# Gated linear attention: a head's states, outputs and their norms one level later among the next head's levels

## The reference

```
b      = cumsum(log_a)                                  # inside a chunk
scores = sum_d q[i,d] k[j,d] exp(b[i,d] - b[j,d]), j<=i
o      = scores @ v + (q * exp(b)) @ h                  # h: state at the chunk's start
h_new  = exp(b_last) * h + (k * exp(b_last - b))^T @ v
o      = rms_norm(o) * silu(g)
```

## Time and profile before

| | |
|---|---|
| median of 3 runs | 2581.73 us (2581.23 to 2584.96) |
| profiled execution | 2579.5 us |
| its span | 2577.7 us |
| PE busy | 2478.8 us (96%) |
| DVE busy | 1064.5 us (41%) |
| ACT busy | 520.0 us (20%) |
| POOL busy | 906.9 us (35%) |
| mean granted clock of TensorE | 0.983 |
| passes of head 1, 2 and 3 | 420.3 to 529.0 us of the span |

### The profile page before, as it was taken

How to read it: one execution, slowest core, us unless ns; L and a number is a source line. 1 busy time by engine, 2 the same in 40 slices (tenths; PEclk the granted TensorE clock), 3 DMA queues, 4 the chain that set the end, 5 groups by cost and what they waited for, 6 DMA issues and landing times.

```text
span 2577.7 us, 40356 instructions
## 1 busy us (share of the span) xinstructions
PE 2478.8 (96%) x16293; PEld 2378.6 (92%) x16293; DVE 1064.5 (41%) x1653; ACT 520.0 (20%) x1118; POOL 906.9 (35%) x449
## 2 busy tenths in 40 slices
PE   7899997889999999999999999999999999999998
PEld 6799987779999999999999888678899999999998
DVE  5322226854633333333335554615533333333333
ACT  5322125441200000000002543123200000000000
POOL 4232333523443343343344421300434334334332
PEclk9999998989999999999999999999999999999999
DMA  6111131231111111111111401410111111111112
GB/s 211 44 33 42 50 123 40 76 139 34 58 42 49 49 41 49 49 41 49 49 42 40 167 31 55 140 67 9 50 50 41 49 49 41 49 49 42 47 42 73
DMA packets 41138, 154.53 MB, mean 60 GB/s; under 512 B 4800, under 2 KB 11584, under 8 KB 38864
## 3 DMA queue, kind: packets, MB, share of 16 engines
q1 hardware_dynamic: 33456, 116.49, 13.9%
q10 hardware_dynamic: 7584, 36.63, 3.7%
HBM read 134.77 MB, written 18.33 MB: 59 GB/s over the span
## 4 chain that ended last, share of the span: by engine, by line
PE 89%; DVE 7%; ACT 2%; issue 2%; DMA 0%; POOL 0%; DVEq 0%; ACTq 0%; SPq 0%; POOLq 0%
PE bank L661 26%; PE bank L663 25%; PE bank L662 25%; PE bank L859 2%; DVE x_lo L1853 1%; PE bank L1285 1%; PE bank L687 1%; PE bank L1258 1%; DVE xt L1843 1%; PE bank L1146 1%; PE bank L1255 1%; PE bank L727 1%; PE bank L747 1%; PE bank L1280 1%; PE bank L735 1%
## 5 line engine op out<-in xcount | busy, mean ns | idle before, releaser
L661 PE MATMUL bank<-x_hi,w_hi 128*128 128x344 f32 (+1 forms) x3272 | 1061.6, 324 | 13.5 <-DVE x_lo L1877 5.4
L662 PE MATMUL bank<-x_lo,w_hi 128*128 128x344 f32 (+1 forms) x3272 | 1046.6, 320 | 0.0
L663 PE MATMUL bank<-x_hi,w_lo 128*128 128x344 f32 (+1 forms) x3272 | 1046.6, 320 | 0.0
L542 POOL TENSOR_TENSOR w_hi<-w_raw,zero 128x1024 fp32r<-128x1024 f32 x176 | 339.7, 1930 | 1455.4 <-PE bank L663 1412.1
L661 PEld LDWEIGHTS bank<-x_hi,w_hi 128*128 128x128 f32 x3272 | 618.9, 189 | 26.3 <-issue 22.8
L662 PEld LDWEIGHTS bank<-x_lo,w_hi 128*128 128x128 f32 x3272 | 618.5, 189 | 2.3 <-issue 0.5
L663 PEld LDWEIGHTS bank<-x_hi,w_lo 128*128 128x128 f32 x3272 | 618.6, 189 | 0.0
L544 POOL TENSOR_TENSOR w_lo<-w_raw,w_hi 128x1024 fp32r<-128x1024 f32 x176 | 433.2, 2462 | 13.8
L2192 DVE TENSOR_TENSOR hid<-sil,bank 128x344 f32<-128x344 f32 x132 | 67.5, 512 | 775.5 <-PE bank L663 740.5
L661 PE MATMUL bank<-hid_hi,w_hi 128*128 128x344 f32 x1056 | 339.6, 322 | 1.2 <-issue 1.2
L663 PE MATMUL bank<-hid_hi,w_lo 128*128 128x344 f32 x1056 | 337.6, 320 | 0.0
(11 more groups left out here) (308 smaller groups left out, 1794.9 us busy)
## 6 DMA issues: line engine op xcount, KB each, us to landing
w_raw<-in_w SPq DMA_DIRECT2D x187, 512.0 KB, 3.4
h<-in_x SPq DMA_DIRECT2D x3, 1376.0 KB, 8.5
h_spill<-h ACTq DMA_DIRECT2D x1, 4128.0 KB, 11.5
h<-h_spill ACTq DMA_DIRECT2D x1, 4128.0 KB, 13.6
out_y<-h ACTq DMA_DIRECT2D x3, 1376.0 KB, 5.6
g_spill<-ring ACTq DMA_DIRECT2D x6, 516.0 KB, 2.6
h<-in_x ACTq DMA_DIRECT2D x1, 3096.0 KB, 10.3
st_ring<-in_state SPq DMA_DIRECT2D x4, 768.0 KB, 5.1
```

Source lines behind the costliest of these rows:

```text
L542: nc.gpsimd.tensor_tensor(w_hi[:, s], w_raw[:, s], zero[:].broadcast_to([P, 1024]), ALU.add).then_inc(s_whi, 1)
L661: pe.matmul(out, wh, xh, start=(i == 0), stop=False)
L662: pe.matmul(out, wh, xl, start=False, stop=False)
L663: mm = pe.matmul(out, wl, xh, start=False, stop=(i == n - 1))
```

## The change

In the three hand-written queues the two halves of `outs` and `outs_normed` go from levels 2 and 3 to levels 3 and 4, and those of `states` from levels 1 and 2 to levels 2 and 3. `outs_turned` and `outs_gated` stay.

```diff
@@ PE's queue
-                        if l in (2, 3):
-                            outs(hh - 1, l - 2)
+                        if l in (3, 4):
+                            outs(hh - 1, l - 3)
                         if l in (5, 6):
                             outs_turned(hh - 1, l - 5)
@@ ACT's queue
-                if l in (2, 3) and hh >= 1:
-                    outs_normed(hh - 1, l - 2)
+                if l in (3, 4) and hh >= 1:
+                    outs_normed(hh - 1, l - 3)
@@ DVE's queue
-                    if l in (1, 2) and hh >= 1:
-                        states(hh - 1, l - 1)
+                    if l in (2, 3) and hh >= 1:
+                        states(hh - 1, l - 2)
```

## The result

The changed kernel takes 2584.59 us (median of 20 runs, 2582.08 to 2588.55), the kernel before, run beside it, 2581.02 (20 runs, 2578.03 to 2584.96). The ratio over the runs is 1.0016 with a 95% interval of 1.0009 to 1.0022 (the medians alone give 1.0014): 3.6 us slower, less than the 0.2% that count as a difference here, but not nothing. The forecast was 2584.2 us and 0.81 for "within 0.2%".

A forecast was written before the change was run, and what follows sets the result against it. TensorE is 96% busy, but in the three changed passes a ring of waits between PE, ACT and DVE bounds; +0.8 us at full clock plus 1.65 for one clock drop gives +2.45 on 2581.73: 2584.2 us, range 2579.6 to 2587.3.

The forecast's parts named there:

- The ring: Heads 1 to 3: ACT waits for PE's outputs (20.2 us), DVE for ACT's decays (10.4), PE for DVE's kept scores.
- Head 1: First pass: level 7 comes 2.1 us earlier, less 0.4 for POOL, leaving 1.7 us where head 2 begins.
- Head 2: Second pass: level 2 still waits for decays behind the sample's norm; lead grows to 2.6 us, adding 0.9.
- Head 3: Third pass: level 7 goes from 524.39 to 525.2, as DVE meets POOL's two splits at level 4.
- the lock: Head 3, level 4: DVE's products and POOL's weight splits exclude each other, a price of 3.3 us, bounds 0 and 3.3.
- the laying-out: The new order timed instruction by instruction through heads 1 to 3; level 4's pair in head 3 takes 4.6 us.
- The clock: PE's idle in front of level 3 or 4 lets TensorE drop to 1.2 GHz: 1.65 us taken, bounds 0 and 5.0.
- The likeliest case: DVE and POOL exclude each other in head 3 and one clock drop shows: 2584.2 us, chance 0.32.
- the second case: DVE and POOL exclude each other in head 3 and two clock drops show: 2585.8 us, chance 0.2.
- The price of 1.65: One clock drop: a level with its outputs takes 5.8 us at 1.2 GHz, 4.2 at 2.4, costing 1.65.
- The three heads together: Sign of being right: heads 1 to 3 take 110 to 112 us, not 108.7.
- What stands behind the passes: Stretches outside 420 to 529 us keep their lengths and only shift; a difference there would show the prediction wrong.

The follow-up runs named there:

- e4: Changed kernel with ACT's norms back in the slots of levels 2 and 3, states and outputs still one level later: 2595.38 us, ratio 1.0058.
- e6: Kernel before with only ACT's norms moved, to the slots of levels 3 and 4: 2578.53 us, ratio 0.9990.
- e9: Changed kernel with the sample's norm on ACT behind level 2's decays in heads 2 and 3: 2580.52 us, ratio 1.0003.
- e11: Kernel before with norms one level later, POOL's split late and the sample's norm behind level 2's decays: 2577.07 us, ratio 0.9988.
- e2: Changed kernel with seven of level 2's products made twice on PE in heads 1 to 3: 2582.76 us, ratio 1.0006.
- e3: Changed kernel with seven level 2 products repeated in heads 1 to 3 and POOL's split behind DVE's last product: 2580.51 us, ratio 1.0001.
- e1: Changed kernel with POOL's split of the weight tile held until DVE has made its last product: 2582.79 us, ratio 1.0010.
- e12: Kernel before run again unchanged, for a second profile: 2580.66 us, ratio 0.9999.
- e8: Kernel before with ACT's norms one level later and POOL's split behind DVE's last product: 2576.79 us, ratio 0.9984.
- e10: Changed kernel with the sample's norm behind level 2's decays in heads 2 and 3, and POOL's split behind DVE's last product: 2579.09 us, ratio 0.9998.
- e7: Kernel before with POOL's split behind DVE's last product: 2580.01 us, ratio 0.9998.

## Why the prediction was right

*The ring.* Right, and e4 and e6 show it: in their old slots behind the later outputs the norms cost 10.8 us, and moved alone they gain 2.2 us in each of heads 1 and 2 and 0.3 in head 3. One mark was wrong: I wrote that ACT's wait ahead of L1537 would shrink. It grew to 26.2 us, because the outputs come later too. What matters is what stands behind it in ACT's queue. DVE's wait for L1564 in front of level 5 went in heads 1 and 2, as written, but came back in front of level 6.

*Head 1.* Forecast 1.7 us of lead at full clock, 0.05 with a fall; measured 0.0 (37.98 against 38.01), with the fall. Level 3 was to start at 433.95 and did at 433.71. The 0.4 us taken off for POOL between level 7 and head 2 came out as 0.5 (451.10 to 458.20, and 451.75 to 458.32 before).

*Head 2.* Forecast 0.9 us of gain at full clock, a loss of 0.75 with a fall; measured a loss of 1.0. That the states had been nearly free in the shade of the sample's norm is shown by e9 and e11 together: with the states behind level 2, taking that norm out of the way gains 3.5 us in this head; with the states ahead of level 2 it gains nothing.

*Head 3.* Forecast 3.4 us of loss with the lock at 3.3; measured 3.1 (31.89 against 28.75), and the pair took 4.4 us where the laying-out said 4.6. The lock alone adds 2.7 us from level 3 to level 7 (18.0 in e2, 15.3 in e3), where the laying-out has 2.95 (525.2 less 522.25). But it isn't 2.7 on top of the fall: taking it away gives back only 1.2 (e1), since the fallen clock stands beneath it. One row was misread: L2008's 2.25 us in the earlier trace rows end at 516.18, half a us behind w_lo (515.64), and not just as it was through. The laying-out of level 4 has that half us all the same.

*The clock.* The likeliest case had one visible fall; the profile has two, in heads 1 and 2, and a third beneath the lock. That is the second case, +4.1 us, and level 7 of head 3 is 4.1 us later. The median of 20 runs, +3.6, lies between the two. That the forecast is within 0.4 us of the measured 2584.59 is part luck: the difference was forecast as 2.45 and came out as 3.6, and the 2581.73 it was added to, a median of 3 runs, lies 0.7 above that of 20. The price of 1.65 is right: 1.66 and 1.61 in e2. The number of falls was the uncertain term, and by this profile 0.32 against 0.2 was weighted the wrong way round: I counted the row of 2.10 us without a fall as much as the two with one.

*The three heads together* were to take 110 to 112 us; they take 112.8.

*What stands behind the passes.* I wrote that the other stretches keep their lengths, and that a difference outside 420 to 529 would speak against me. In the two profiles 2.1 of the 6.1 us lie behind level 7 of head 3. I have no account of them from the prediction. The kernel before differs from itself by 1.6 us in such a stretch (e12), so they may be the run's and not the edit's.

*Open.* The leads at level 7 of head 3 are larger than those of the medians: 4.8 us and 1.5 in e6, 6.35 and 3.2 in e8, 4.3 and 0.5 in e10. The stretch between the two products named at e12 runs the same instructions in all kernels and took from 1063.4 us (e6, e12) to 1069.1 (e10), 1066.9 in the changed kernel. Of e10's 4.1 us over the first profile of before, PE's idle time is 1.2; the rest goes with a lower clock, as over these 50 us of the window attention (first before, then e10):

```profile
1650.20:1700.20 50.00, 47.90 (x485) 35.50 (x483) 13.96 (x25) 12.69 (x27) 0.00 (x0) 0.97 0.38 149
```
```profile
1645.00:1695.00 50.00, 47.90 (x453) 35.06 (x450) 14.02 (x25) 11.60 (x25) 0.00 (x0) 0.86 0.37 147
```

In the changed kernel the clock over the whole stretch is as low as before, and most of the 1.9 us is idle time of PE (1.4; both are estimates from PE's busy time and granted clock in twelve windows). Whether a shifted start of the stage brings this about or chance does, one profile a kernel does not tell, and it was not tried. Nor were the outputs moved by themselves, without norms and states.

## What to carry to other kernels

When work is moved later in one engine's queue, ask of every engine what filled the place it leaves: here the norms were worth moving (they stood in front of a decay that others needed), the outputs were the filling of a gap on TensorE, and the states lay in the shade of another wait. Split such a change into its engines' parts before judging it: one line of three gave a gain, all three a loss. A wait that goes from a trace is gone only if it does not return a level later.

## What the runs showed of the hardware

- How long TensorE's idle is does not by itself say whether the clock falls behind it. In e7 it fell behind 1.76 us, in level 7 of head 2; in e4 it stayed up behind 3.01 us, in level 6 of head 3:

```profile
491.60 3.48 PE L862 MATMUL bank<-q_a,k_a 128*128 128x128 f32 x16 [1.76 <-DVE s_acc L2030]
```
```profile
536.62 2.05 PE L859 MATMUL bank<-dqk 128*128 128x128 f32 x16 [3.01 <-DVE s_acc L2029]
```

- The same idle of 2.09 or 2.10 us, in front of level 7 of head 0 in all 14 profiles, let the clock fall in four of them (that level then took 3.65 to 3.67 us, not 2.05). It isn't shown to be chance: in these four (e2, e6, e7, e8) the level starts latest in the span, at 410.01 to 410.36 us, and in the ten others at 407.48 to 409.50. What decides is open. Seven repeated products in such a gap made heads 1 and 2 shorter by 1.7 and 1.6 us (e2).
- DVE's product with two operands in SBUF and POOL's instructions alternate whole instruction by whole instruction: 1.68 and 2.83 us for two of 0.68. Beside copies of scores and additions of states from banks POOL's instructions kept their 1.04 to 1.06 us (509.20 and 510.20 in the changed kernel). The Trainium skill, "SBUF — State Buffer", section "Who interferes with whom", says that a DVE instruction with two inputs in SBUF contends with a GpSimd instruction that reads SBUF, and one with at most one such input, outside its two-port modes, does not. The trace agrees with both, and adds that a pair of short instructions can pay for both of POOL's long ones.
- Copying the kept scores (L2029, the same 128x256 elements a time) took 1.3 us for two at levels 0 and 1 and 0.75 at all coarser ones, with and without POOL beside it.
